# Gate rows of an mLSTM layer laid out as 64 rows of 128 in place of 8 rows of 1024

## What is computed

```python
log_f = log_sigmoid(f_pre)                 # min(f, 0) - log(1 + exp(-|f|))
# per head, chunk after chunk; m is the stabiliser carried between chunks
bcum = cumsum(log_f)                       # restarts in every chunk
m_t = max(bcum + m, running max of (bcum_t - bcum_s + log_i_s))
w_inter = exp(bcum + m - m_t)              # weight of the carried state
floor = exp(-m_t)                          # lower bound of the denominator
m_new = max(bcum[-1] + m, max(bcum[-1] - bcum + log_i))
w_c = exp(bcum[-1] + m - m_new); w_s = exp(bcum[-1] - bcum + log_i - m_new)
```

## Time and profile before

| | us |
|---|---|
| median of 3 runs (1392.82 to 1394.35) | 1393.07 |
| the profiled execution | 1397.93 |
| its span, first to last instruction | 1396.2 |
| PE busy | 1381.0 (99%) |
| DVE busy | 1162.0 (83%) |
| ACT busy | 764.3 (55%) |
| POOL busy | 153.9 (11%) |

### The profile page before, as it was taken

How to read it: one execution, slowest core, us unless ns; L and a number is a source line. 1 busy time by engine, 2 the same in 40 slices (tenths; PEclk the granted TensorE clock), 3 DMA queues, 4 the chain that set the end, 5 groups by cost and what they waited for, 6 DMA issues and landing times.

```text
span 1396.2 us, 19118 instructions
## 1 busy us (share of the span) xinstructions
PE 1381.0 (99%) x6608; PEld 1155.4 (83%) x6608; DVE 1162.0 (83%) x1886; ACT 764.3 (55%) x1336; POOL 153.9 (11%) x250
## 2 busy tenths in 40 slices
PE   9999999999999999999999999999999999999997
PEld 7888888888888888888888888778888888888886
DVE  7989989898999989899874445797888888889976
ACT  6875766747576675757743435664333333336340
POOL 2002011110201111010000001001111111100021
PEclk9999999999999999999999999999999999999999
DMA  5114334252433426245497666334666555689661
GB/s 230 46 41 136 98 97 138 73 176 62 136 99 100 135 61 171 77 137 174 131 329 248 221 195 223 129 108 117 157 166 161 152 148 153 175 256 360 214 204 76
DMA packets 103439, 213.31 MB, mean 153 GB/s; under 512 B 10912, under 2 KB 27552, under 8 KB 102192
## 3 DMA queue, kind: packets, MB, share of 16 engines
q1 hardware_dynamic: 90544, 178.53, 38.1%
q0 software_dynamic: 12800, 33.56, 12.5%
HBM read 170.04 MB, written 75.56 MB: 176 GB/s over the span
## 4 chain that ended last, share of the span: by engine, by line
PE 86%; DVE 8%; DMA 3%; issue 1%; ACT 1%; POOL 0%; SPq 0%; DVEq 0%; ACTq 0%; POOLq 0%
PE wide L2930 19%; PE wide L2932 19%; PE wide L2931 19%; PE ps_state L2930 3%; PE ps_state L2931 3%; PE ps_state L2932 3%; PE ps_inter L2931 2%; PE ps_inter L2930 2%; PE ps_inter L2932 2%; PE ps_intra L3110 2%; PE ps_intra L2931 1%; PE ps_intra L2930 1%; PE ps_s L2930 1%; PE ps_s L2931 1%; PE ps_intra L2932 1%; PE ps_s L2932 1%
## 5 line engine op out<-in xcount | busy, mean ns | idle before, releaser
L2931 PE MATMUL wide<-xa,inb 128*128 128x512 f32 x576 | 224.7, 390 | 0.0
L2930 PE MATMUL wide<-xb,inb 128*128 128x512 f32 x472 | 189.7, 402 | 2.2 <-DVE z_buf L1977 1.5
L2932 PE MATMUL wide<-xb,inb 128*128 128x512 f32 x472 | 184.4, 391 | 0.0
L2931 PEld LDWEIGHTS wide<-xa,inb 128*128 128x128 f32 x576 | 108.4, 188 | 20.1
L2931 PE MATMUL wide<-xa,blk 128*128 128x512 f32 x320 | 124.5, 389 | 0.0
L2930 PEld LDWEIGHTS wide<-xb,inb 128*128 128x128 f32 x472 | 88.8, 188 | 20.9 <-issue 2.7
L2932 PEld LDWEIGHTS wide<-xb,inb 128*128 128x128 f32 x472 | 88.6, 188 | 19.2
L2930 PE MATMUL wide<-xb,blk 128*128 128x512 f32 x256 | 99.6, 389 | 0.0
L2932 PE MATMUL wide<-xb,blk 128*128 128x512 f32 x256 | 99.6, 389 | 0.0
L1859 ACT ACTIVATE wy<-wy_raw 128x1024 fp32r<-128x1024 f32 x56 | 59.3, 1061 | 62.3 <-DMA wy_raw<-y_block 62.1
L2557 DVE TENSOR_TENSOR mw<-mw_raw,mw 128x1024 fp32r<-128x1024 f32 x53 | 63.3, 1221 | 24.8 <-ACT mw L1705 24.7
(11 more groups left out here) (449 smaller groups left out, 3984.5 us busy)
## 6 DMA issues: line engine op xcount, KB each, us to landing
in_raw<-in_w_in SPq DMA_DIRECT2D x45, 512.0 KB, 4.3
wy_raw<-y_block SPq DMA_DIRECT2D x56, 256.0 KB, 4.4
mw_raw<-h_block SPq DMA_DIRECT2D x53, 256.0 KB, 3.3
m_sum<-in_w_out POOLq DMA_DIRECT2D x48, 256.0 KB, 4.2
h_block<-f_buf SPq DMA_DIRECT2D x48, 256.0 KB, 2.9
w_sum<-in_pool_w_out POOLq DMA_DIRECT2D x48, 256.0 KB, 4.3
a_raw<-in_pool_w_z SPq DMA_DIRECT2D x16, 512.0 KB, 4.1
a_raw<-folded SPq DMA_DIRECT2D x16, 512.0 KB, 4.3
```

Of the source, the lines that this page charges most:

```text
L2930: pe.matmul(dst, a[0], b[0], start=first, stop=False, skip_group_check=more)
L2931: pe.matmul(dst, a[0], b[1], start=False, stop=False, skip_group_check=more)
L2932: return pe.matmul(dst, a[1], b[0], start=False, stop=last, skip_group_check=more)
```

## The change

The gate rows are kept as 64 rows (8 heads by 8 chunks) of 128 tokens. Three things are new. The summed gates in `kT` go to DRAM by two DMAs and come back by two others in the new shape. The maximum that is carried from chunk to chunk is no longer found by a scan over 1024 tokens: each row is scanned by itself, the last sum and the last maximum of each row are turned from partitions to columns by 32 by 32 transposes on DVE, a scan over 36 elements carries the maximum through the chunks of four heads at a time, a third transpose turns the starting values back, and one pass applies them. The exponentials become one pass each with a bias per partition. PE transposes two tiles in place of eight, and `gcol` has another order of its axes. SP's lines, the memsets of POOL (two of 64 rows by 128 and two small ones, in place of three of 1024 columns and a small one) and the lists of ACT and DVE in the opening are adapted.

```diff
+            sp.wait_ge(gate_vec, VEC_SUM)
+            sp.dma_start(g_rows[1, :, :], kT[LF, :]).then_inc(rows_out, 16)
+            sp.dma_start(g_rows[0, :, :], kT[HI, :]).then_inc(rows_out, 16)
+            sp.wait_ge(rows_out, 32)
+            sp.dma_start(f_row, by_unit(g_rows[1, :, :])).then_inc(gate_in, 16)
+            sp.dma_start(i_row, by_unit(g_rows[0, :, :])).then_inc(gate_in, 16)
             sp.wait_ge(gate_vec, VEC_M)
-            sp.dma_start(m_rows, m_row).then_inc(rows_out, 16)
+            sp.dma_start(by_unit(m_rows), m_row).then_inc(rows_out, 16)
...
-            sp.wait_ge(gate_act, ACT_ROWS)
             load_rows(0)
...
             def abs_log_gates():
-                act.wait_ge(gate_vec, VEC_SUM)
+                act.wait_ge(gate_in, 64)
...
             def gate_weights():
                 act.wait_ge(gate_vec, VEC_ROWS)
-                gate(act.activation(rows[64:64 + HEADS, :], lf_row, ACT.Exp, scale=-1.0))
-                for c in range(NC):
-                    gate(act.activation(rows[LF, tile(c)], m_row[:, tile(c)], ACT.Exp, scale=-1.0,
-                                        bias=m_prev[:, c:c + 1]))
-                gate(act.activation(w_chunk, by_chunk(rows[LF, :])[:, :, CHUNK - 1], ACT.Copy))
+                gate(act.activation(inter, m_row, ACT.Exp, scale=-1.0, bias=m_prev))
...
             def last_weights():
-                for c in range(NC):
-                    gate(act.activation(rows[96:96 + HEADS, tile(c)], rows[HI, tile(c)], ACT.Exp,
-                                        bias=m_last[:, c:c + 1]))
+                gate(act.activation(floor, m_full, ACT.Exp, scale=-1.0))
+                gate(act.activation(source, rest, ACT.Exp, bias=m_last))
...
-                gate(dve.tensor_tensor_scan(bcum, keep, lf_row, 0.0, ALU.mult, ALU.add))
+                gate(dve.tensor_tensor_scan(bcum, ones, lf_row, 0.0, ALU.mult, ALU.add))
             def running_max():
-                gate(dve.tensor_tensor(rows[HI, :], i_row, bcum, ALU.subtract))
-                gate(dve.tensor_copy(by_chunk(carry)[:, 1:NC, 0], by_chunk(bcum)[:, 0:NC - 1, CHUNK - 1]))
-                gate(dve.tensor_tensor_scan(m_row, carry, rows[HI, :], 0.0, ALU.add, ALU.max))
+                gate(dve.tensor_tensor(rest, i_row, bcum, ALU.subtract))
+                gate(dve.tensor_tensor_scan(m_own, zeros, rest, -FAR, ALU.add, ALU.max))
+                gate(dve.transpose(sum_end, bcum[:, CHUNK - 32:CHUNK]))
+                gate(dve.transpose(max_end, m_own[:, CHUNK - 32:CHUNK]))
+                gate(dve.tensor_copy(step_sum[:, :, 1:NC + 1], by_end(sum_end)))
+                gate(dve.tensor_tensor(step_max[:, :, 1:NC + 1], by_end(sum_end), by_end(max_end), ALU.add))
+                gate(dve.tensor_tensor_scan(start_flat, step_flat, max_flat, 0.0, ALU.add, ALU.max))
+                gate(dve.tensor_copy(by_end(start_rows), m_start[:, :, 0:NC]))
+                gate(dve.transpose(m_col, start_rows))
+                gate(dve.tensor_scalar(m_row, m_own, m_prev, None, ALU.max))
                 assert gates[0] == VEC_M
...
-                gate(dve.tensor_tensor(lf_row, bcum, m_row, ALU.add))
+                gate(dve.tensor_tensor(m_full, bcum, m_row, ALU.add))
+                gate(dve.tensor_scalar(m_last, m_row[:, CHUNK - 1:CHUNK], -1.0, None, ALU.mult))
...
-                for c in range(NC):
-                    mm = pe.transpose((ps_state, ps_inter)[c // 4][:, tile(c % 4)], rows[:, tile(c)], ident[:, :])
+                for m, b in enumerate((ps_state, ps_inter)):
+                    mm = pe.transpose(b[:, 0:P], qT[:, tile(m)], ident[:, :])
```

More of the change, by code:

```diff
@@ L434, in build, with row_slot @@
         HI_TOO, LF_TOO = slice(64, 64 + HEADS), slice(96, 96 + HEADS)
[L435 to L438, removed]
+        UNITS_G = slice(0, HEADS * NC)
+        UPPER = slice(HEADS * NC, 2 * HEADS * NC)
+        def row_slot(at, i):
+            return qT[at, i * CHUNK:(i + 1) * CHUNK]
+        rest, inter, floor, source = row_slot(UNITS_G, 0), row_slot(UPPER, 0), row_slot(UNITS_G, 1), row_slot(UPPER, 1)
+        f_row, f_abs, lf_row, bcum = (row_slot(UNITS_G, i) for i in range(2, 6))
+        m_row, m_full = row_slot(UNITS_G, 6), row_slot(UNITS_G, 7)
+        ahead = f_buf[UNITS_G, 0, :]
+        i_row, ones, zeros, m_own = (ahead[:, i * CHUNK:(i + 1) * CHUNK] for i in range(4))
+        sum_end, max_end = ahead[:, 512:544], ahead[:, 544:576]
+        step_sum, step_max, m_start = (ahead[:, at:at + 36].rearrange("p (h c) -> p h c", c=NC + 1) for at in (576, 612, 648))
+        step_flat, max_flat, start_flat = (ahead[:, at:at + 36] for at in (576, 612, 648))
+        start_rows, m_col = ahead[:, 704:736], ahead[:, 736:768]
+        m_prev, m_last = m_col[:, 31:32], ahead[:, 768:769]
         gate_rest = m_bc
-        carry, keep = f_buf[HI, 0, :], f_buf[HI, 1, :]
-        m_prev, m_last = small[HI, 0, :], small[HI, 1, :]
-        w_chunk = small[LF, 2, :]
         def x_piece(n):
@@ L1032, in _ @@
                 lambda: pool.memset(g_raw[:, :, :], 0.0),
[L1033 to L1036, removed]
+                lambda: pool.memset(ones, 1.0),
+                lambda: pool.memset(zeros, 0.0),
+                lambda: pool.memset(step_sum[:, :, 0:1], -FAR),
+                lambda: pool.memset(step_max[:, :, 0:1], 0.0),
                 lambda: pool.memset(small[:, :, :], 0.0),
@@ L1311, in gcol_at @@
             def gcol_at(c, q, h):
[L1312 removed]
+                return gcol[:, q, h, c:c + 1]
             def decay(h, c):
@@ L1639, in _ @@
             take_v(0, 2)
-            in_high(15)
+            take_v(0, 3)
+            take_q(0, 0)
             in_high(16)
-            take_q(0, 0)
             take_q(0, 1)
-            tanh_z(0, 1)
-            take_v(0, 3)
             take_k(0, 0)
+            weighted_k(0, 0)
             take_k(0, 1)
-            tanh_o(0, 0)
-            weighted_k(0, 0)
             round_s(0, 0)
@@ L1653, in _ @@
             in_snapshot(3, 1)
+            tanh_o(0, 0)
             in_high(17)
@@ L2059, in scales @@
                 step(dve.scalar_tensor_tensor(out=big, in0=num[:, part, DV], scalar=-1.0,
-                                              in1=gcol[:, part, 2, h], op0=ALU.mult, op1=ALU.max), wait=False)
+                                              in1=gcol[:, 2, h, part], op0=ALU.mult, op1=ALU.max), wait=False)
                 for c in range(4 * f, 4 * f + 4):
@@ L2429, in _ @@
             operand_sum(0)
-            operand_sum(1)
             low_gates()
             operand_lo(8)
+            operand_sum(1)
             operand_lo(9)
-            in_low(4)
+            low_qkv(0)
+            scale_columns()
             operand_sum(2)
             operand_sum(3)
-            in_sum(2, 0)
             operand_sum(4)
-            in_low(5)
-            scale_columns()
             operand_sum(5)
             operand_sum(6)
+            in_low(4)
+            in_low(5)
+            in_low(6)
             tap(0, 1, 1)
@@ L2447, in _ @@
             gate_sum(1)
-            in_low(6)
-            in_low(7)
             operand_lo(10)
             operand_lo(11)
+            operand_lo(12)
             operand_sum(7)
+            tap(0, 0, 1)
+            in_sum(2, 0)
+            in_low(7)
             log_gates()
             running_max()
-            low_qkv(0)
+            gate_conv(0, 1)
             in_low(8)
+            in_low(9)
+            operand_lo(13)
+            operand_lo(14)
             in_sum(2, 1)
[L2458 to L2461, removed]
             in_sum(2, 2)
             in_sum(2, 3)
-            operand_lo(13)
-            operand_lo(14)
             operand_lo(15)
@@ L2496, in _ @@
             in_sum(3, 2)
+            weighted_s(0, 1)
+            gate_out_z(0, 1)
+            low_k(0, 1)
+            low_s(0, 1)
             next_state(0, 0)
-            weighted_s(0, 1)
-            low_s(0, 1)
-            low_k(0, 1)
+            low_v(0, 2)
+            in_low(17)
             chunk_stats(0, 0)
-            in_low(17)
-            low_v(0, 2)
             for h in range(1, HEADS):
```

90 lines of the change are left out of this document (46 added, 44 removed).

## The result

The changed kernel takes 1397.02 us, the median of 14 runs (1395.27 to 1398.55), and the kernel before on the same chips 1393.84, the median of 14 (1391.76 to 1395.12). The ratio is 1.002, with a 95% interval of 1.0013 to 1.0027: by the ratio 2.8 us slower (the two medians are 3.2 us apart), where 2.0 us less was predicted. The profiled execution after is the fastest of its 14, 1395.27 with a span of 1393.4 us.

A forecast was written before the change was run, and what follows sets the result against it. PE, busy 99%, bounds the kernel; DVE's list binds the opening, by only 1.3 us. Two stalls (0.84, 0.43), slow matmuls (0.17) and transposes (0.6) sum to 2.0 us less: median 1391.0 us, range 1389.7 to 1393.1.

The forecast's parts named there:

- The DVE block: Gate work on DVE: 8.96 us become fourteen dependent instructions of 4.0 us, 5.5 with dear transposes; DVE gets back 5.0 us.
- the end near the small copy: DVE's 64 by 32 transposes: price between 0.16 us (smallest copy) and 0.69 (512-column pass), taken as 0.2.
- The trip through DRAM: Summed gates stored and reloaded after `gate_sum(1)`: rows there at 46.8 us, 44.5 to 49.1; DVE idle for 2.9 us.
- rival A: Opening: only the transposes pay, the stalls return elsewhere after a longer DRAM trip; gain 0.6 us, 1392.5; chance 0.20.
- the 2.3 us that `in_low(10)` had to spare: DVE's list in the opening: `in_low(10)` done at 61.8 us, PE wants it at 64.14.
- The transposes and the first stall: PE's opening: the 0.84 us wait ahead of (2, 6) goes; eight transposes become two, 0.6 us less.
- the slow matmul behind the old stall: PE's first matmul after each of two stalls is some 0.1 us slow; 0.17 us counted as gain for both.
- Edits at nothing: POOL's memsets, `gcol`'s order and the 4-byte `w_c` store cost nothing; `wc_bc` load lands at 67.2, 3.6 us to spare.
- The 1.4 us that I had to spare at (2, 5): Opening: DVE's `operand_lo(17)` ends at 68.4 us, PE comes to product (2, 5) at 69.8.
- B: Rival: slower than before, as a DRAM trip over 10 us makes PE wait for product (2, 1); 1396.2; chance 0.06.
- C: Rival: gain over 2.8 us, half of PE's 1.75 us loss over the heads could go; 1389.9; chance 0.14.
- The rest of the forecast: After the opening: `values(0)` starts near 72.5 us, and PE's lead of 2.0 us is kept through the heads.

The follow-up runs named there:

- experiment 3: Changed kernel with `w_c` stored from `gcol` as one 256-byte piece, behind `load_in(3, 0)` and head 0's rows, two waits moved; 1393.03 us, ratio 0.9989 to the kernel before.
- 4: Changed kernel with the `w_c` store in its place but as 64 pieces of 512 bytes (output wrong); 1391.66 us, ratio 0.9977 to the kernel before.
- 5: Changed kernel with the `w_c` store in its place but as 64 pieces of 128 bytes (output wrong); 1392.38 us, ratio 0.9991 to the kernel before.
- 10: Repeat of experiment 3 with no further edit; 1392.57 us, ratio 0.9993 to the kernel before.
- experiment 7: Kernel before with its `w_c` store cut into 64 pieces of 4 bytes in place of 8 of 32; 1393.11 us, ratio 0.9989 to the kernel before.
- experiment 8: Kernel before with the changed lists of ACT and DVE but the old gate rows; 1401.76 us, ratio 1.0042 to the kernel before.

## Why the prediction was wrong, step by step

**The DVE block: right.** Fourteen instructions run from 47.28 to 51.21, 3.9 us for 4.0. A scan over 128 took 0.42 for 0.41, over 36 0.22, a transpose 0.20: the end near the small copy was the right one. The Trainium skill's 311 ns (VectorE: DVE Perf Modes, The three transpose paths) is for a larger tile in bf16; the 64 by 32 tile in fp32 here took 0.20 us.

**The trip through DRAM: right in kind, a little pessimistic.** SP issued the loads at 41.7, so a store of 32 KB lands within 2.1 us. ACT starts at 44.91, for 46.8 worked out and 44.5 as the low end. It didn't wait for the rows, as the forecast said it would: it had waited 4.39 us for DVE's `operand_sum(7)` and came to them behind `operand_hi(13)`, so they may have landed earlier. DVE's wait was 0.84 us for 2.9. Two sizes were off without harm: ACT's passes without a bias took 0.29 to 0.31 us for 0.44, and in rival A a trip 2.3 us longer would only use up the 2.3 us that `in_low(10)` had to spare, not miss by 0.4.

**The transposes and the first stall: right.** (2, 6) has no stall, and the 0.6 us of the transposes are there (0.13 us from the first transpose to the next product, for 0.79: 0.66 less). With the slow matmul behind the old stall that makes the lead at 66.88, 1.75 us for the 1.5 worked out (0.84, 0.1 and 0.6).

**Edits at nothing: the step that failed.** It said of the 4-byte store that it lands within 3.1 us, that the load of `wc_bc` is back at 67.2, and that 3.6 us are to spare in all. The store alone was back only at 67.1 (6.8 us; 8.1, 7.1 and 7.5 in the other runs), 3.7 us or more beyond its bound. The bound of 3.1 came from a store of 8 pieces of 32 bytes and was used for 64 pieces of 4, though the same text says that no run shows such a store's price. An unknown price asks for both ends and a rival of its own; I gave it one end, the friendly one.

**What was queued behind it: overlooked.** I counted DVE's wait for `wc_bc` as the only reader. The load issued 0.7 us behind the store became the first thing to be late (9.2 us in place of 3.9), and `load_rows(0)` behind SP's wait the second. The 1.4 us that I had to spare at (2, 5) were those of DVE's `operand_lo(17)`; what ACT had to spare there I hadn't counted. In experiment 3 its snapshot ends at 67.87, and PE came to (2, 5) at 69.75 in the changed kernel, so it was 1.9 us. ACT came 3.5 us late, and the other 1.6 are the stall of the trace.

**The rivals.** B had the right side with the wrong DMA: it put the danger on the trip of the gates, whose loads have pieces of 512 bytes, and that trip took at most 5.6 us in all, from 39.27 to 44.91. It named the small store and let it go. The rule that it quoted, the Trainium skill's (DMA: Bandwidth & Descriptors, Specifications) that transfers under 512 B are read-modify-writes, gives no time. The runs show a cost at 4 bytes and none at 128 (at most 1.8 us, against 1.9 at 512), so taken as a threshold for time it doesn't hold here; whether such a read and write back is what made the 4-byte store slow, no run shows. C's mechanism shows in the traces, its size not in the times: between 120 and 650 us PE lost 0.1 to 0.4 us in experiments 3, 4, 5 and 10, and 1.75, 3.5 and 0.7 in the three profiles of the kernel before and experiment 7.

**The rest of the forecast** was met once the store was out of the way: `values(0)` starts at 72.3 to 72.8 for 72.5, and the heads kept PE's lead, as the table shows. That the mean ratio, 0.9988, came so near to 0.9985 is partly luck, since repeats and equal openings differ by 0.0004 to 0.0014.

## What to carry to other kernels

When a layout changes, look at the small DMAs that follow from it: what were eight rows of eight numbers became a column of 64, and its pieces of 4 bytes decided the result, not its 256 bytes in all. Price such a transfer by its pieces, list what is issued behind it and who waits behind SP for it, and where no row has its like, give it a rival with a time. A slow transfer that cost nothing had cover; a change that makes the engines earlier takes that cover away.

## What the hardware showed that I had not expected

A store of 64 pieces of 4 bytes took 6.8, 8.1, 7.1 and 7.5 us in four executions, from two tiles; 64 pieces of 128 or 512 bytes took at most 1.9, and one piece of 256 bytes at most 1.1. A load of 512 KB behind the former landed after 9.2, 10.6 and 8.8 us, and after 3.9 ahead of it, and in the changed kernel the engines moved 66 GB/s at a busy share of 1.39 meanwhile. What the engines do in that time wasn't tried.

A wait of 3.7 us in experiment 8 was followed by a granted clock of 0.50 and cost PE 2.4 us on top of itself.

PE's wait in the heads for DVE's `in_join` differs between executions of one kernel: 1.5 and 3.0 us in two of the kernel before and 0.6 in experiment 7, 0.7 and 0.5 in two of the changed one. What sets these waits stays open.
